# Attention regrouped into 36 phases of 1024 score columns a head, value products moved ahead of the transposes

## The chip, the cores and the metric

The kernel runs on one core of one Trainium2 chip. The metric is the time of one execution on the device, in microseconds. Instructions are issued in order on each engine: TensorE (matrix products and transposes, results to PSUM), VectorE (DVE), ScalarE (ACT), GpSimd (POOL) and SyncE (SP, which only starts transfers). Engines wait for each other by semaphores that count up.

## What is computed

The reference is one layer of a hybrid decoder for 1024 tokens of 1024 channels. The change touches the softmax and the value products of its two attention branches, which come between the input projection and the output projections:

```python
# branch B, causal, 8 heads; q, k of 64 + 32 channels
logits = einsum('bqhd,bshd->bhqs', q, k) * 96 ** -0.5
logits = where(s_idx <= t, logits, -inf)
y_b    = einsum('bhqs,bshd->bqhd', softmax(logits), v)      # v of 64 channels
# branch A, 8 query heads on 2 key heads, 64 channels; only the 256 keys that an indexer picks
logits = einsum('bqcgd,bqncd->bqcgn', q, k_sel) * 64 ** -0.5 - slope * distance
y_a    = einsum('bqcgn,bqncd->bqcgd', softmax(logits), v_sel)
merged = sigmoid(ga) * (y_a @ w_pa) + sigmoid(gb) * (y_b @ w_pb)
```

In the kernel branch A is dense and causal too: a table `sc` of what is to be subtracted holds the distance, and a huge number where a key isn't picked.

## The kernel before

The tokens are eight blocks of 128. Query block i sees i + 1 key blocks, `KEYS[i]` = 128 (i + 1) columns. Heads go in pairs p = 0 to 3; e = 0, 1 is the head in the pair, and the two heads' score products run in the two halves of TensorE's rows. A *step* n is one (branch, query block i, pair p). `STEPS` lists 64 of them, first 32 of branch B, then 32 of branch A; block 4 alternates with block 3, then 5 with 2, 6 with 1, 7 with 0:

```python
ORDER = [(TT - 1 - g, g) for g in reversed(range(TT // 2))]
STEPS = [(br, i, p) for br in "BA" for big, small in ORDER for p in range(PAIRS) for i in (big, small)]
```

For each step five things happen:

- **scores** (`scores_b` L2507 and L2511: five products per head; `scores_a` L2528: three) into two PSUM banks a head, in pieces of at most 512 columns;
- **reduction** on DVE (L1921): it writes scores minus mask into a buffer `prob` in SBUF and gives the row maximum; a short TENSOR_SCALAR (L1923 in B, L1926 in A) makes of it `shift`, and counts `shift_ready`. From then on the score banks are free;
- **exponential** on ACT (L1430), in place in `prob`, counted by `prob_ready`;
- **transposes** (`turn_probs`, L2544): 128 x 128 each, into units of up to four in a ring of three PSUM banks (`RING`), each unit counted by `turned`; ACT (L1394) or DVE (L1882, `copy_turned`) copies each unit to `prob_t`. A unit needs the one three before it to be copied;
- **value products** (`sum_values`, L2558), one per key block and head, which need all copies of their step; they count `pv_done`, and ACT takes the result out of PSUM (L1413, `take_y`).

TensorE's loop n issues scores(n), then transposes(n-1), then value products(n-2). DVE's loop n does both heads' reductions of n, then its copies of n-1. ACT's loop n does `take_y`(n-3) and then, for each head, its copy of n-1 and its exponential of n. There are four `prob` buffers, two for the even steps and two for the odd, so that a reduction of step n needs the transposes of step n-2.

Some work is laid into the same loops at given n: the split of `ka` into a high and a low part (`KA_SPLIT_AT`, ACT L1435 and DVE L1933) and of the queries `qa` of each set of blocks (`QA_SPLIT_AT`, L1439 and L1938), the inverse of branch B's sums (`INV_B`, `turn_inverse` L2569), and its spreading over the heads with the scaling of `yb` (`SPREAD_B`, four times: `spread_inverse` L2580 on TensorE, `scale_y` L1899 on DVE; they use the same ring). The same for branch A comes after the last step, `turn_inverse("A")` inside loop N + 1. Then the output products begin (L2282, `yb_hi`).

Of the kernel before, what the change touches and what calls it, by code (L numbers as in the profile page):

```python
# [22 lines left out]
P = 128  # L23
# [4 lines left out]
ALU = mybir.AluOpType  # L28
# [3 lines left out]
HEADS, HEAD_DIM = 8, 64  # L32
# [66 lines left out]
def build(nc, x, p, positions, g_mix, w_in, g_cq, w_uq, g_ckv, w_ukv, w_pa, w_pb, w_out, g_mlp, w_ff1, w_ff2,  # L99
# [36 lines left out]
    with ctx:  # L136
# [84 lines left out]
        PROB_AT = [(0, S), (4, S), (8, HALF), (10, HALF)]  # L221
        prob_b = [at(f"prob_b{j}", T + o * K, [n]) for j, (o, n) in enumerate(PROB_AT)]
        prob_a = [at(f"prob_a{j}", NX + (12 + o) * K, [n]) for j, (o, n) in enumerate(PROB_AT)]
        prob_tb = [at(f"prob_tb{j}", R1 + o * K, [n]) for j, (o, n) in enumerate(PROB_AT)]
        prob_ta = [at(f"prob_ta{j}", NX + o * K, [n]) for j, (o, n) in enumerate(PROB_AT)]
# [41 lines left out]
        max_c = col("max", 4)  # L267
        shift_c = col("shift", 4)
        fin_c = rstd_c = max_c
# [337 lines left out]
        NB = N // 2  # L607
        BANK_BLOCKS = HALF // P
# [32 lines left out]
        def turn_units(n):  # L641
            return [(e, half, UNIT_AT["turn", n, e, half]) for e in range(2)
                    for half in range(2) if ("turn", n, e, half) in UNIT_AT]
# [4 lines left out]
        def tiles_of(i, half):  # L648
            return (0, min(BANK_BLOCKS, i + 1)) if half == 0 else (BANK_BLOCKS, i + 1)
# [16 lines left out]
        KA_SPLIT_AT = 8  # L666
        QA_SPLIT_AT = [NB - 6, NB + 4, NB + 11, NB + 17]

# [4 lines left out]
        def prob_of(n, e):  # L673
            return (prob_b if STEPS[n][0] == "B" else prob_a)[2 * (n % 2) + e]

        def prob_t_of(n, e):
            return (prob_tb if STEPS[n][0] == "B" else prob_ta)[2 * (n % 2) + e]

# [12 lines left out]
        def y_steps(br, p):  # L691

            return 1 + max(n for n, (b, _, q) in enumerate(STEPS) if (b, q) == (br, p))

# [2114 lines left out]
```

## Time and profile before

| | |
|---|---|
| median of 3 runs | 1650.67 us (1650.38 to 1651.82) |
| the profiled execution | 1650.06 us, of which its span is 1648.3 us |
| mean granted TensorE clock | 0.996 of full |
| TensorE busy over the span | 97% |
| attention, branch B | about 433 to 580 us |
| attention, branch A | about 580 to 706 us |

The span runs from the first to the last instruction of the profile; 1.76 us of the execution lie around it. The profile has one row for each instruction or run of like instructions, with its start, its length and the idle time of its engine before it, and what ended it. A matmul's length is longer than its place in the pipeline: the distance from one start to the next is its cost. PEld rows are the weight loads that go before each matmul; they show those distances best.

### The profile page before, as it was taken

What the parts mean: (1) busy time and instruction counts of PE and PEld (TensorE: products, weight loads), DVE (VectorE), ACT (ScalarE), POOL (GpSimd) and SP (SyncE); (2) the same over time, 40 slices, a digit from 0 to 9 for tenths busy, and PEclk for the clock granted to TensorE, in tenths of its full rate; (3) what the DMA queues carried; (4) which work ended last, traced back from release to release, by engine and by line L of the source; (5) the groups of instructions that cost most, each with busy time, mean ns of one, the idle gap of its engine ahead of it and who ended that gap; (6) DMA issues with size and microseconds to landing.
All of it is one profiled execution on the core that took longest, in us unless ns stands there. A gap on an engine that the chain in (4) does not pass through costs nothing.

```text
span 1648.3 us, 23187 instructions
## 1 busy us (share of the span) xinstructions
PE 1596.7 (97%) x8576; PEld 1296.1 (79%) x8576; DVE 1201.2 (73%) x1851; ACT 699.9 (42%) x1151; POOL 637.1 (39%) x397
## 2 busy tenths in 40 slices
PE   6999999999999999999999999999999999999997
PEld 5778888787777777778888788888878888888786
DVE  7679999982656677754354777776699999898445
ACT  5432422323566677621144443343354444444223
POOL 2222532213200002012213545445589888885230
PEclk9999999999999999999999999999999999999999
DMA  5312223243300010203442354555494544422112
GB/s 164 93 39 58 96 77 102 90 126 82 90 1 2 1 40 2 78 25 131 168 137 89 119 169 141 160 171 160 155 338 170 204 163 166 141 90 64 45 58 102
DMA packets 115240, 177.46 MB, mean 108 GB/s; under 512 B 19104, under 2 KB 73376, under 8 KB 115008
## 3 DMA queue, kind: packets, MB, share of 16 engines
q1 hardware_dynamic: 111296, 162.44, 30.2%
q10 hardware_dynamic: 3680, 13.63, 2.2%
q8 instruction: 64, 1.05, 0.3%
q14 instruction: 40, 0.33, 0.1%
q0 software_dynamic: 160, 0.02, 0.0%
HBM read 123.24 MB, written 49.68 MB: 105 GB/s over the span
## 4 chain that ended last, share of the span: by engine, by line
PE 87%; DVE 7%; ACT 3%; issue 2%; POOL 1%; DMA 1%; SPq 0%; ACTq 0%; DVEq 0%
PE ps L2282 35%; PE ps L2718 18%; PE ps L2677 17%; PE ps L2544 3%; PE ps L2558 2%; PE ps L2507 2%; PE ps L2528 2%; PE ps L2423 2%; DVE prob_a L1921 1%; PE ps L2362 1%; PE ps L2330 1%; DVE prob_b L1921 1%; PE ps L2511 1%; PE ps L2641 1%; PE ps L2384 1%
## 5 line engine op out<-in xcount | busy, mean ns | idle before, releaser
L1037 POOL TENSOR_TENSOR w_lo<-w_raw,w_hi 128x1024 fp32r<-128x1024 f32 x67 | 166.1, 2480 | 481.9 <-ACT w_hi L1187 481.9
L1106 POOL TENSOR_TENSOR a_lo<-s_raw,a_hi 128x512 fp32r<-128x512 f32 x128 | 189.8, 1490 | 95.2 <-ACT a_hi L1466 94.8
L1187 ACT ACTIVATE w_hi<-w_raw 128x1024 fp32r<-128x1024 f32 x67 | 70.9, 1059 | 343.0 <-PE ps L2282 275.3
L2677 PE MATMUL ps<-b_hi,a_hi 128*128 128x512 f32 x448 | 175.3, 391 | 3.7 <-POOL a_lo L1106 1.7
L2718 PE MATMUL ps<-b_hi,a_hi 128*128 128x512 f32 x448 | 174.5, 390 | 2.4 <-DVE h L2155 2.4
L2677 PE MATMUL ps<-b_hi,a_lo 128*128 128x512 f32 x448 | 174.4, 389 | 0.0
L2677 PE MATMUL ps<-b_lo,a_hi 128*128 128x512 f32 x448 | 174.3, 389 | 0.0
L1106 POOL TENSOR_TENSOR a_lo<-f_raw,a_hi 128x512 fp32r<-128x512 f32 x96 | 136.8, 1439 | 97.1 <-ACT a_hi L1466 97.0
L2718 PE MATMUL ps<-b_lo,a_hi 128*128 128x512 f32 x448 | 174.3, 389 | 0.0
L2718 PE MATMUL ps<-b_hi,a_lo 128*128 128x512 f32 x448 | 174.3, 389 | 0.0
L2282 PE MATMUL ps<-n_hi,w_hi 128*128 128x512 f32 x544 | 168.3, 391 | 2.4 <-ACT rel L1247 1.3
L1769 DVE TENSOR_SCALAR_CACHE_REDUCE tested<-sc,bar_i 128x384 bf16<-128x384 f32 (+2 forms) x192 | 169.0, 942 | 1.7 <-POOL sc L1052 0.6
L2282 PE MATMUL ps<-n_hi,w_lo 128*128 128x512 f32 x544 | 167.5, 389 | 0.0
L2282 PE MATMUL ps<-n_lo,w_hi 128*128 128x512 f32 x544 | 167.4, 389 | 0.0
L2155 DVE TENSOR_TENSOR h<-h,ps 128x512 f32<-128x512 f32 x224 | 142.8, 677 | 23.4 <-PE ps L2718 23.0
L2105 DVE TENSOR_TENSOR b_lo<-b_lo,b_hi 128x512 fp32r<-128x512 f32 x112 | 143.5, 1321 | 0.1
L2282 PEld LDWEIGHTS ps<-n_hi,w_hi 128*128 128x128 f32 x544 | 101.8, 188 | 25.2 <-ACT rel L1247 1.7
L2282 PEld LDWEIGHTS ps<-n_lo,w_hi 128*128 128x128 f32 x544 | 102.1, 188 | 21.2
L2282 PEld LDWEIGHTS ps<-n_hi,w_lo 128*128 128x128 f32 x544 | 102.1, 188 | 21.2
L1466 ACT ACTIVATE a_hi<-s_raw 128x512 fp32r<-128x512 f32 x128 | 78.7, 627 | 92.5 <-PE ps L2718 90.9
L2677 PEld LDWEIGHTS ps<-b_hi,a_hi 128*128 128x128 f32 x448 | 84.1, 188 | 23.3 <-POOL a_lo L1106 3.3
L2718 PEld LDWEIGHTS ps<-b_hi,a_hi 128*128 128x128 f32 x448 | 84.1, 188 | 21.0 <-issue 3.5
(356 smaller groups left out, 3224.4 us busy)
## 6 DMA issues: line engine op xcount, KB each, us to landing
f_raw<-in_w_ff_dram SPq DMA_DIRECT2D x64, 512.0 KB, 4.3
b_lo<-hid_scratch SPq DMA_DIRECT2D x112, 256.0 KB, 5.5
hid_scratch<-c_out SPq DMA_DIRECT2D x32, 512.0 KB, 3.7
w_raw<-in_w_in_dram SPq DMA_DIRECT2D x28, 512.0 KB, 3.7
hid_scratch<-t_out SPq DMA_DIRECT2D x15, 768.0 KB, 6.1
gates_scratch<-stage ACTq DMA_DIRECT2D x16, 512.0 KB, 3.4
sig_ab<-gates_scratch SPq DMA_DIRECT2D x8, 1024.0 KB, 5.9
x_tok<-in_x_dram SPq DMA_DIRECT2D x8, 512.0 KB, 10.1
```

The costliest lines, as they stand in the source:

```text
L1037: pool.tensor_tensor(lo_of(first)[:, :, :], w_raw[s][:, :, :], hi_of(first)[:, :, :].bitcast(F32), ALU.subtract).then_inc(lo_ready, 1)
L1106: pool.tensor_tensor(slot(a_lo, o), first_of(o), slot(a_hi, o).bitcast(F32), ALU.subtract).then_inc(a_lo_done, 1)
L1187: act.activation(hi_of(first)[:, :, :], w_raw[s][:, :, :], ACT.Copy).then_inc(hi_ready, 1)
L1466: act.activation(slot(a_hi, o), first_of(o), ACT.Copy).then_inc(a_hi_done, 1)
L1769: ins = dve.tensor_scalar(tested[:, at0:at0 + KEYS[i]], s_i, bar_f[:, f:f + 1], None, ALU.is_ge, ALU.add, accum_out=count_c[:, f:f + 1])
L1921: link(dve.tensor_tensor_reduce(prob_of(n, e)[:, 0:w], s, less, 1.0, LOWEST, ALU.subtract, ALU.max, top))
L2105: dve.tensor_tensor(b_lo[r][:, b, :], b_lo[r][:, b, :].bitcast(F32), b_hi[r][:, b, :].bitcast(F32), ALU.subtract).then_inc(hid_lo_done, 1)
L2155: dve.tensor_tensor(h[k][:, part], h[k][:, part], pair_bank(w, name, ab), ALU.add).then_inc(added, 1)
L2282: last = pe.matmul(bank(4 * half + 2 * j + t)[0:w, :], wm, xm[:, t * HALF:(t + 1) * HALF], start=(n == 0 and a), stop=(n == total - 1 and ...
L2544: last = pe.transpose(bank(u % RING)[:, (k - k0) * P:(k - k0 + 1) * P], prob_of(n, e)[:, k * P:(k + 1) * P], ident[:, :])
L2677: last = pe.matmul(unit_bank(u, PLACE[name]), w[o % NS][:, j, :], x[j][:, b, :], start=name in ("P1", "P2", "P5") and j == 0 and a, stop=j ...
L2718: last = pe.matmul(pair_bank(w, name, ab), x[(LAST + o) % NS][:, 2 * j + ab, :], y[r][:, b, :], start=name in ("P1", "P2", "P5") and j == ...
```

## The change

The work of a branch is cut into 18 *phases* of exactly eight key blocks (1024 score columns) a head, instead of 32 steps of one to eight. A phase has one or two *members* (query block, pair, first column). Blocks 4 and 2 (5 + 3 key blocks) share a phase, 5 and 1 (6 + 2), 6 and 0 (7 + 1); block 7 fills a phase alone; block 3 of two pairs (4 + 4) fills one. Reductions, exponentials and `take_y` still go by member. TensorE's loop n now issues scores(n), value products(n-2), transposes(n-1). ACT's loop n takes the exponentials of the second members after both of the first. There are three `prob` buffers of 1024 columns a branch, used in turn by head: `prob` of phase n, head e is number (2n + e) mod 3. The units of transposes come in the order (first half, e = 0), (first half, e = 1), (second half, e = 0), (second half, e = 1); ACT copies the first two, DVE the last two, always 512 columns. `shift` has eight columns instead of four and takes the maximum in place.

The core of the diff; left out are renamings in `scores_a` (as in `scores_b`) and the counts of a few waits outside the attention:

```diff
-        prob_b = [at(f"prob_b{j}", T + o * K, [n]) for j, (o, n) in enumerate(PROB_AT)]
-        prob_a = [at(f"prob_a{j}", NX + (12 + o) * K, [n]) for j, (o, n) in enumerate(PROB_AT)]
+        prob_b = [at(f"prob_b{j}", T + 4 * j * K, [S]) for j in range(3)]
+        prob_a = [at(f"prob_a{j}", NX + (12 + 4 * j) * K, [S]) for j in range(3)]
+        prob_tb = [at(f"prob_tb{j}", R1 + 4 * j * K, [S]) for j in range(4)]
...
-        max_c = col("max", 4)
-        shift_c = col("shift", 4)
+        shift_c = col("shift", 8)
...
-        ORDER = [(TT - 1 - g, g) for g in reversed(range(TT // 2))]
-        STEPS = [(br, i, p) for br in "BA" for big, small in ORDER for p in range(PAIRS) for i in (big, small)]
+        ORDER = [(4, 2), (5, 1), (6, 0), (7, 3)]
+        def members_of(set_):
+            big, small = ORDER[set_]
+            if set_ < len(ORDER) - 1:
+                return [[(big, p, 0), (small, p, KEYS[big])] for p in range(PAIRS)]
+            return [[(big, p, 0)] for p in range(PAIRS)] + [[(small, p, 0), (small, p + 1, KEYS[small])] for p in (0, 2)]
+        STEPS = [(br, set_, members) for br in "BA" for set_ in range(len(ORDER)) for members in members_of(set_)]
...
-        INV_B = NB + 4
+        INV_B = NB + 2
         SPREAD_B = [INV_B + 2 + p for p in range(PAIRS)]
         for n in range(1, N + 1):
-            br, i, p = STEPS[n - 1]
-            for e in range(2):
-                add_unit("act" if i >= BANK_BLOCKS or e == 0 else "dve", "turn", n - 1, e, 0)
-                if i >= BANK_BLOCKS:
-                    add_unit("dve", "turn", n - 1, e, 1)
+            for half in range(2):
+                for e in range(2):
+                    add_unit("dve" if half else "act", "turn", n - 1, e, half)
...
-        KA_SPLIT_AT = 8
-        QA_SPLIT_AT = [NB - 6, NB + 4, NB + 11, NB + 17]
+        KA_SPLIT_AT = 5
+        QA_SPLIT_AT = [NB - 4, NB + 2, NB + 6, NB + 9]
...
         def prob_of(n, e):
-            return (prob_b if STEPS[n][0] == "B" else prob_a)[2 * (n % 2) + e]
+            return (prob_b if n < NB else prob_a)[(2 * n + e) % 3]
...
-        YB_HI_AT = [NB + 11 + 2 * k for k in range(YT)]
+        YB_HI_AT = [NB + 8 + k for k in range(YT)]
...
+                if n < N and len(MEMBERS[n]) == 2:
+                    for e in range(2):
+                        exponents(n, 1, e)
...
+                for a, e in itertools.product(range(len(MEMBERS[n]) if n < N else 0), range(2)):
...
+                    top = shift = shift_c[:, m % 8:m % 8 + 1]
                     dve.wait_ge(s_ready[e], n + 1)
-                    if n % NB >= 2:
-                        dve.wait_ge(turned, turned_after(n - 2, e))
+                    before = 2 * n + e - 3
+                    if a == 0 and before >= 2 * (n // NB * NB):
+                        dve.wait_ge(turned, turned_after(before // 2, before % 2))
...
+            def scores_free(n, e, at0):
+                if n >= 1 and at0 == 0:
+                    pe.wait_ge(shift_ready, score_index(n - 1, 0, e) + 1)
+                if n >= 1 and at0 == HALF:
+                    pe.wait_ge(shift_ready, 2 * FIRST_M[n])
...
             def turn_probs(n):
                 for e, half, u in turn_units(n):
-                    pe.wait_ge(prob_ready, 2 * n + e + 1)
+                    pe.wait_ge(prob_ready, probs_at(n, e, half))
                     unit_free(u)
...
             for n in range(1, N + 2):
-                if n == 4:
+                if n == 2:
                     pe.wait_ge(q_moved, ROPE_MOVED[1])
...
                 if n == 1:
                     freed(pe, 0, values_free)
+                if n >= 2:
+                    sum_values(n - 2)
                 if 1 <= n <= N:
                     turn_probs(n - 1)
                 if n == INV_B:
                     turn_inverse("B")
                 if n in SPREAD_B:
                     spread_inverse("B", SPREAD_B.index(n))
                 if n == N + 1:
                     turn_inverse("A")
-                if n >= 2:
-                    sum_values(n - 2)
```

`score_index(n, a, e)` numbers the reductions in their order, `FIRST_M[n]` is the number of members before phase n, `turned_after(n, e)` the count at which all units of that phase and head are transposed. So the first head of a phase may be reduced once the second head of the phase two before is transposed, and its second head once the first head of the phase just before is.

## Rows read from the trace of the kernel before

**Rows 1.** The page's first part: busy us of each engine, its share of the span, instructions.

```profile
PE 1596.7 (97%) x8576; PEld 1296.1 (79%) x8576; DVE 1201.2 (73%) x1851; ACT 699.9 (42%) x1151; POOL 637.1 (39%) x397
```

**Rows 2.** Windows over the two halves of the attention: start:end, length, busy us of each engine.

```profile
433.00:580.00 147.00, 137.56 (x1345) 108.40 (x1344) 84.75 (x243) 95.76 (x216) 4.70 (x2) 0.98 0.08 21
580.00:706.00 126.00, 118.73 (x1205) 91.14 (x1204) 89.78 (x260) 90.44 (x221) 9.86 (x5) 1.00 0.11 35
```

**Rows 3.** Waits in the attention, 433 to 706 us: who waited for whom, total, times, longest.

```profile
DVE prob_b L1921 <- PE ps L2511: 45.3, 29, 2.8
...
DVE prob_a L1921 <- PE ps L2528: 20.8, 25, 1.7
```

**Rows 4.** Timeline of branch A, TensorE's lines: start us, us, engine, line, operation.

```profile
657.17 0.50 PE L2528 MATMUL ps<-ka_hi,qa_hi 64*128 64x512 f32 x2
...
657.74 0.40 PE L2528 MATMUL ps<-ka_hi,qa_lo 64*128 64x512 f32 x2
...
657.97 0.33 PE L2528 MATMUL ps<-ka_hi,qa_hi 64*128 64x384 f32 x2
...
658.59 0.42 PEld L2544 LDWEIGHTS ps<-ident,prob_a 128*128 128x128 f32 x4 [0.26 <-issue]
...
659.18 1.51 PEld L2558 LDWEIGHTS ps<-prob_ta,va 128*64 128x64 f32 x28 [0.17 <-issue]
...
661.29 0.18 PEld L2528 LDWEIGHTS ps<-ka_hi,qa_hi 64*128 64x128 f32 x1 [0.25 <-DVE cols L1926]
...
661.84 1.18 PEld L2544 LDWEIGHTS ps<-ident,prob_a 128*128 128x128 f32 x11
...
664.37 0.50 PE L2528 MATMUL ps<-ka_hi,qa_hi 64*128 64x512 f32 x2
```

**Rows 5.** The same stretch, VectorE's lines.

```profile
658.70 1.09 DVE L1921 CUSTOM_DVE_ANT_0 prob_a<-ps,sc 128x896 f32<-128x896 f32 x1 [1.38 <-PE ps L2528]
...
659.95 1.09 DVE L1921 CUSTOM_DVE_ANT_0 prob_a<-ps,sc 128x896 f32<-128x896 f32 x1
...
661.08 0.15 DVE L1926 TENSOR_SCALAR cols<-cols 128x1 f32<-128x1 f32 x1
...
661.84 0.42 DVE L1921 CUSTOM_DVE_ANT_0 prob_a<-ps,sc 128x256 f32<-128x256 f32 x1 [0.25 <-PE ps L2528]
...
662.42 0.42 DVE L1921 CUSTOM_DVE_ANT_0 prob_a<-ps,sc 128x256 f32<-128x256 f32 x1
...
663.96 0.56 DVE L1882 COPY prob_ta<-ps 128x384 f32<-128x384 f32 x1 [0.43 <-PE ps L2544]
```

**Rows 6.** Timeline of branch B, VectorE's lines around a reduction of 1024 columns.

```profile
546.34 0.21 DVE L1923 TENSOR_SCALAR cols<-cols 128x1 f32<-128x1 f32 x1
...
549.89 0.69 DVE L1882 COPY prob_tb<-ps 128x512 f32<-128x512 f32 x1 [0.19 <-PE ps L2544]
```

**Rows 7.** First scores of step 1, first of branch A, first product after the attention.

```profile
441.70 0.18 PEld L2507 LDWEIGHTS ps<-kn_hi,qn_hi 64*128 64x128 f32 x2 [0.35 <-issue]
...
578.78 0.19 PEld L2528 LDWEIGHTS ps<-ka_hi,qa_hi 64*128 64x128 f32 x2 [0.17 <-issue]
...
705.80 0.30 PEld L2282 LDWEIGHTS ps<-yb_hi,w_hi 128*128 128x128 f32 x2 [0.17 <-issue]
```

**Rows 8.** Timeline around the split of ka, step 8 of the kernel before.

```profile
478.34 2.29 DVE L1933 TENSOR_TENSOR ka_lo<-ka,ka_hi 128x2048 fp32r<-128x2048 f32 x1 [2.40 <-ACT ka_hi L1435]
...
481.41 0.28 PEld L2507 LDWEIGHTS ps<-kn_hi,qn_hi 64*128 64x128 f32 x1 [1.12 <-DVE cols L1923]
```

**Rows 9.** Windows of 1 us behind it; PEclk is the granted clock behind POOL's.

```profile
482.00:483.00 1.00, 1.00 (x5) 0.78 (x6) 0.73 (x3) 1.00 (x4) 0.00 (x0) 0.50 0.00 0
...
488.00:489.00 1.00, 1.00 (x22) 0.83 (x18) 0.33 (x1) 1.00 (x4) 0.00 (x0) 1.00 0.00 0
```

**Rows 10.** The last transposes of the kernel, and a window among them.

```profile
1631.19 3.71 PE L2784 MATMUL ps<-ident,h 128*128 128x128 f32 x32
...
1638.00:1640.00 2.00, 1.52 (x12) 1.29 (x13) 1.93 (x5) 1.97 (x5) 0.00 (x0) 1.00 0.97 391
```

More of the change, by code:

```diff
@@ L641, in turn_units, with score_index, probs_at @@
         def turn_units(n):
-            return [(e, half, UNIT_AT["turn", n, e, half]) for e in range(2)
-                    for half in range(2) if ("turn", n, e, half) in UNIT_AT]
+            return [(e, half, UNIT_AT["turn", n, e, half]) for half in range(2) for e in range(2)]
         def turned_after(n, e):
             return 1 + max(u for e2, _, u in turn_units(n) if e2 == e)
-        def tiles_of(i, half):
-            return (0, min(BANK_BLOCKS, i + 1)) if half == 0 else (BANK_BLOCKS, i + 1)
+        def score_index(n, member, e):
+            return 2 * (FIRST_M[n] + member) + e
+        def probs_at(n, e, half):
+            last = max(a for a, (_, _, c0) in enumerate(MEMBERS[n]) if c0 < (half + 1) * HALF)
+            return score_index(n, last, e) + 1
         HI_ORDER = [("qi", 0), ("qn", 0), ("qn", 1), ("kr", 0), ("qr", 0), ("qn", 2), ("qn", 3), ("qr", 1)]
@@ L1410, in take_y, with exponents @@
             def take_y(n):
-                br, i, p = STEPS[n]
                 act.wait_ge(pv_done, n + 1)
-                act.activation(y_of(br)[:, p, i * P:(i + 1) * P], bank(PV_BANK)[:, 0:P],
-                               ACT.Copy).then_inc(y_copied, 1)
+                for a, (i, p, _) in enumerate(MEMBERS[n]):
+                    last = act.activation(y_of(STEPS[n][0])[:, p, i * P:(i + 1) * P], bank(PV_BANK)[:, a * P:(a + 1) * P],
+                                          ACT.Copy)
+                last.then_inc(y_copied, 1)
+            def exponents(n, a, e):
+                br = STEPS[n][0]
+                i, p, c0 = MEMBERS[n][a]
+                m, hd = score_index(n, a, e), 2 * p + e
+                act.wait_ge(shift_ready, m + 1)
+                prob = prob_of(n, e)[:, c0:c0 + KEYS[i]]
+                act.activation(prob, prob, ACT.Exp, bias=shift_c[:, m % 8:m % 8 + 1],
+                               scale=q_norm[:, i:i + 1] if br == "B" else SLOPES[hd],
+                               accum_out=sums_of(br)[:, i, hd:hd + 1]).then_inc(prob_ready, 1)
             for n in range(N + 3):
@@ L2539, in turn_probs @@
                 for e, half, u in turn_units(n):
-                    pe.wait_ge(prob_ready, 2 * n + e + 1)
+                    pe.wait_ge(prob_ready, probs_at(n, e, half))
                     unit_free(u)
-                    k0, k1 = tiles_of(STEPS[n][1], half)
-                    for k in range(k0, k1):
-                        last = pe.transpose(bank(u % RING)[:, (k - k0) * P:(k - k0 + 1) * P],
-                                            prob_of(n, e)[:, k * P:(k + 1) * P], ident[:, :])
+                    for k in range(BANK_BLOCKS):
+                        at0 = half * HALF + k * P
+                        last = pe.transpose(bank(u % RING)[:, k * P:(k + 1) * P], prob_of(n, e)[:, at0:at0 + P], ident[:, :])
                     last.then_inc(turned, 1)
             def sum_values(n):
-                br, i, p = STEPS[n]
+                br = STEPS[n][0]
                 for _, _, u in turn_units(n):
```

134 lines of the change are left out of this document (61 added, 73 removed).

## The prediction

> **What bounds the kernel now.** I read the page's first part, then windows over the attention, its waits, and the timeline of single steps. TensorE is busy 97% of the span [rows 1], and in the attention it stays the busiest engine: 137.6 of 147 us in branch B and 118.7 of 126 in A, where DVE has 89.8 and ACT 90.4 [rows 2]. So DVE waits for TensorE's scores, 45.3 us in B and 20.8 in A [rows 3], and TensorE waits little. But "busy" includes the drain of matmuls. The timeline shows what a step costs TensorE: a pair of blocks, nine key blocks a head, takes 664.37 - 657.17 = 7.20 us in A [rows 4]. Its own work by distances between starts is less. 28 weight loads of value products take 1.51 us, 0.054 each; 11 transposes take 1.18, 0.107 each; a score product of both heads takes 657.97 - 657.74 = 0.23 for 512 columns and, from 657.97 to 658.59 less the 0.10 of a change of kind, three of 384 in 0.52, 0.175 each [rows 4]. For 256 and 128 columns I estimate 0.12, between a load's 0.107 and the (661.84 - 661.29 - 0.10)/3 = 0.15 that a stretch of 256 with its start took. At a change of kind (scores, transposes, value products) 0.10 to 0.17 us goes idle. Work of the pair: scores 1.57, 18 transposes 1.93, 36 loads 1.94, in all 5.4; the remaining 1.8 us are six changes and short waits. This remainder is what fewer phases could save.
>
> **What the change removes.** The number of transposes, value products, pieces of scores and reductions is the same: per pair set, 5 + 4, 6 + 3, 7 + 2, 8 + 1 blocks become 5 + 3, 6 + 2, 7 + 1, 8, 4 + 4, with 48 pieces a branch either way. ScalarE and VectorE copy 512 columns always; that is no more than now in sum. Changes of kind fall from 3 x 64 to 3 x 36, and if nothing else bound, a phase would cost TensorE in A: scores 1.4, value loads 32 x 0.054 = 1.73, transposes 16 x 0.107 = 1.71, changes 0.45, in sum 5.3 us; in B, with five products, 6.3.
>
> **What it adds: a wait of VectorE within the loop.** The second head of phase n takes the `prob` buffer of the first head of phase n - 1, which must be transposed first. TensorE does this after the scores of n and after the value products of n - 2. Take V as the start of value products in loop n. The third unit of the transposes is the one waited for: value products 1.73, change 0.17, eleven transposes 1.18, and from the start of a unit's last transpose to DVE about 0.45 (the next scores start at 664.37; less 0.17, eight loads 0.43 and 0.17 the last transpose began near 663.5, and the copy of it starts at 663.96 [rows 4, 5]). The reductions after the first thus start at V + 3.5, where DVE had been free since about V + 1.3. Bounds 3.3 and 3.7.
>
> From there I follow DVE. The distance from one reduction to the next is 1.25 for 896 columns and 0.58 for 256 [rows 5], so 0.31 + 0.00105 w: 0.45, 0.58, 0.71, 0.85, 0.98, 1.12, 1.25, 1.38 for one to eight blocks; B has 0.02 more, its TENSOR_SCALAR being 0.21 instead of 0.15 [rows 5, 6]. TensorE is released 0.10 after the last distance in A (661.08 + 0.15, then 661.29), 0.15 in B. Two things hang on it.
>
> *Scores.* Pieces of phase n + 1 that begin at column 512 wait for all reductions of n; the tail behind that wait is five products in B, three in A. Loop time = 3.5 + three reductions + 0.15 + tail + 0.10. B: blocks 5 + 3: 3.5 + 2.46 + 0.15 + 1.45 + 0.10 = 7.66; 6 + 2: 3.5 + 2.34 + 0.15 + 1.2 + 0.1 = 7.29; 7 + 1: 7.41; 4 + 4: 3.5 + 2.61 + 0.15 + 1.15 + 0.1 = 7.5. Block 8 alone has one reduction (1.40), after which all of the second head's scores, 2.2, remain: 7.35.
>
> *Copies.* DVE copies units three and four after its reductions: 0.62 + 0.69 [rows 6] and 0.06 to TensorE, which needs them for the next value products. In A this is later than the scores: 5 + 3: 3.5 + 2.40 + 1.37 = 7.27; 6 + 2: 7.15; 7 + 1: 7.02; 4 + 4: 7.42. Block 8 alone is held by scores, 3.5 + 1.38 + 0.10 + 1.35 + 0.10 = 6.43.
>
> ScalarE fits in: after its first copy near V + 2.5 it has four exponentials and a copy, done by V + 7, and TensorE wants them at V' + 1.9, V' being the next V.
>
> **The sum.** Step 1's scores start at 441.70 [rows 7]; block 2's piece in phase 0 moves that by 0.3, as the wait for the value copies hides the rest. Scores(1) end at 444.6, the first third unit is through at 446.3, reductions 2.46, 0.15, tail 1.45: V of loop 2 is 450.4. Loops 2 to 17: 2 x 7.6 + 4 x 7.3 + 4 x 7.4 + 4 x 7.35 + 2 x 7.5 = 118.4. The split of `ka` (2.29 us on DVE, after ScalarE's high part [rows 8]) comes between two phases and delays the first reduction beyond V + 3.5: 1.6. Loop 18 starts at 570.4, its scores at 569. Now they start at 578.8 [rows 7]: B gains 10, of which 5 is a stall that the same split causes now.
>
> A: loop 18 needs no buffer back (`before` is below the branch), 5.4; three loops of 7.27; four of 7.15; four of 7.02; four of 6.43; two of 7.42: 124.4 with it. The inverse and the four spreads of B sit behind the transposes in the ring; their second unit needs DVE's copy of the third unit, which now comes at V + 3.5 + 2.3 + 0.7 = V + 6.5, and the next scores only after: 8.4 and 8.7 instead of 7.15 and 7.27, 6.4 in all. Last, value products of the last two phases, transposes, copies, then `turn_inverse("A")`: 7.8 (1.73 + 0.17 + 1.6 + 0.45, copies 1.0, value products 1.73, inverse 1.1). 570.4 + 124.4 + 6.4 + 7.8 = 709.0, against 705.8 now [rows 7]: **+3.2 us**. `qa` splits, `scale_y` and the inversion on DVE cost nothing: they lie between the copies and V + 3.5, where DVE waits 2 us a loop; without that cover each would cost its 0.7 to 1.3. SP's loads wait for counts reached as early as now. After the attention nothing changes.
>
> **The clock.** In the split's stall now, TensorE did little from 477.6 to 481.4, then was granted half clock: 0.50 in the window at 482, 1.00 again in that at 488 [rows 8, 9]. That was about 6.5 us, and a stretch at half clock costs at most half of itself. In the new loops with an inverse or a spread TensorE has nothing but two short instructions from V + 3.6 to V + 6.5, and in the `ka` loop little over 2.8 us. Six such places, each at least as empty as that stall; I count two to three drops of 2 us each, bounds 0 and 6 x 3.3. [...]
>
> Normal loops idle less at a time (1.0 + 0.8 + 0.4 us in A) but have 1.7 us of transposes before it. Transposes alone kept the clock at the end of the kernel: from 1631.19 on there is nothing else, and the window at 1638 has 1.00 [rows 10]. [...]
>
> **The rivals.**
> 1. *The clock holds.* The sum alone: 1650.06 + 3.2 = 1653, no change that a measurement can tell (below 0.2%, 3.3 us). For it: in A now it stayed at 1.00 [rows 2].
> 2. *Faster: the buffer is not what holds.* If the third unit were through before DVE ends its first reduction (V + 1.3), phases would cost 6.3 and 5.3: 16 x 1.1 + 17 x 1.7 = 46 us less, near 1607. The point from which it decides: at a gate of V + 3.5 every loop is bound by it; at V + 3.25 the sum is already 8 us lower, 1645. Against it: the order of the three parts on TensorE fixes the gate by work that I priced from rows.
> 3. *Half clock through much of the attention.* At half clock a loop's gate comes 1.4 later and its tail 0.7 to 1: if the 17 loops of A ran so, +35, near 1690.
> 4. *Nothing lost in the special loops*, because the ring's units are free earlier than I count: -6, near 1652 with the clock drops.
>
> **How the numbers follow.** The likeliest: the sum with two to three drops, 1650.06 + 3.2 + 5 = 1658.3; the profiled execution is 0.6 below the median of the runs, which I ignore: 1658. Chances: forecast 0.45, clock holds 0.20, ring free 0.10, faster 0.13, half clock 0.12. The gate's bounds are worth +-6 us over 33 loops. The range 1642 to 1675 leaves out the ends of rivals 2 and 3. Forecast alone: 1651 to 1668. Faster 0.16 (rival 2 and the low end of 1 and 4), same 0.24, slower 0.60.
>
> **What would show it.** Right: in A a loop of 7.0 to 7.3 us from value products to value products; each second head's reduction waits about 2 us for a transpose (L2544's counterpart), some 65 us over the attention; scores on TensorE released by DVE's TENSOR_SCALAR, value products by DVE's copy; B's scores end about 10 us earlier, the first output product 3 to 8 later; half clock only near 475 to 510 or 590 to 640. Wrong: loops of 6.3 and 5.3, TensorE waiting for nothing, or a clock below 1.00 in plain loops.

## The result and the profile after

| | before | after |
|---|---|---|
| median of 4 runs each | 1650.53 us (1650.37 to 1651.82) | 1677.16 us (1675.74 to 1679.02) |
| ratio | | 1.016, 95% interval 1.0143 to 1.0178 |
| span of the profiled execution | 1648.3 us | 1675.5 us |
| mean granted TensorE clock | 0.996 | 0.991 |

The change makes the kernel 26.6 us slower. The direction of the prediction was right; the size (1658) was not, and the time lies past the end of the range (1675).

The first part of the page after, against [rows 1]: TensorE's busy time is 3 us more, but its share falls from 97 to 95%.

```profile
PE 1599.9 (95%) x8576; PEld 1303.9 (78%) x8576; DVE 1200.5 (72%) x1827; ACT 688.4 (41%) x1127; POOL 636.9 (38%) x397
```

Windows over branch B and branch A (columns as in [rows 2]). In A the engine is busy for 130 of 161.5 us, and the clock has come down to 0.94.

```profile
433.00:571.50 138.50, 128.49 (x1292) 102.97 (x1290) 81.98 (x222) 86.11 (x194) 4.73 (x2) 1.00 0.08 22
571.50:733.00 161.50, 129.85 (x1257) 103.10 (x1257) 92.98 (x260) 87.85 (x218) 9.71 (x5) 0.94 0.08 27
```

The first output product, against the last row of [rows 7]:

```profile
732.81 0.30 PEld L2294 LDWEIGHTS ps<-yb_hi,w_hi 128*128 128x128 f32 x2
```

It comes 732.81 - 705.80 = 27.0 us later: the whole loss lies in the attention.

The waits of the attention, 433 to 735 us, against [rows 3]. L1932 is the reduction, L2565 the transposes, L1404 ScalarE's copy of them, L1935 and L1938 the short instruction behind a reduction, L2580 the value products, L1420 `take_y`, L1895 VectorE's copy.

```profile
ACT prob_ta L1404 <- PE ps L2565: 64.5, 19, 7.0
ACT prob_tb L1404 <- PE ps L2565: 51.3, 17, 3.7
DVE prob_a L1932 <- PE ps L2565: 48.9, 17, 4.1
...
DVE prob_b L1932 <- PE ps L2565: 35.1, 17, 2.7
...
PEld ps L2527 <- DVE cols L1935: 15.2, 24, 1.0
...
PE ps L2580 <- ACT ya L1420: 6.9, 5, 2.4
PE ps L2580 <- DVE prob_ta L1895: 5.9, 5, 3.5
...
PE ps L2580 <- ACT yb L1420: 3.2, 2, 1.9
```

VectorE's reductions wait for transposes, 48.9 + 35.1 = 84 us, where they waited for scores before. ScalarE's copies wait for transposes for 116 us; it is the other engine on which a loop can hang. And TensorE's value products wait for ScalarE's `take_y`, 6.9 + 3.2 = 10.1 us in seven waits, a pair that the prediction doesn't have. In the kernel before, 433 to 706 us, the same wait (L2558 for L1413) is next to nothing:

```profile
PE ps L2558 <- ACT ya L1413: 0.7, 2, 0.5
```

In what follows V is the start of a loop's value products, as in the prediction, and the *gate* is the wait of the second head's reduction for its `prob` buffer, which the third unit of transposes ends. One loop of branch B, from value products to value products, is 544.29 - 536.69 = 7.60 us:

```profile
536.69 1.73 PEld L2580 LDWEIGHTS ps<-prob_tb,vb 128*64 128x64 f32 x32 [0.35 <-issue]
...
538.59 1.29 PEld L2565 LDWEIGHTS ps<-ident,prob_b 128*128 128x128 f32 x12 [0.17 <-issue]
...
540.26 1.23 DVE L1932 CUSTOM_DVE_ANT_0 prob_b<-ps,mask 128x1024 f32<-128x1024 f32 x1 [2.20 <-PE ps L2565]
...
541.80 0.18 PEld L2527 LDWEIGHTS ps<-kn_hi,qn_hi 64*128 64x128 f32 x1 [0.98 <-DVE cols L1935]
...
543.02 0.42 ACT L1420 ACTIVATE yb<-ps 128x128 f32<-128x128 f32 x2
...
544.29 1.29 PEld L2580 LDWEIGHTS ps<-prob_tb,vb 128*64 128x64 f32 x24 [0.35 <-issue]
```

The second head's reduction starts at V + 3.57 after a wait of 2.20 us for the third unit of transposes (predicted V + 3.5), TensorE's next scores are released 1.54 later, and the tail takes 2.49. This is the predicted loop, 0.25 longer. `take_y` is done at 543.44, 0.85 before the value products: it fits in here.

Once in B it does not. ScalarE's part of the split of `ka` stands before `take_y`, and the value products wait 1.90 us for that; the loop is 9.38 us instead of 7.6:

```profile
480.82 1.90 ACT L1450 ACTIVATE ka_hi<-ka 128x2048 fp32r<-128x2048 f32 x1
...
483.18 1.97 PE L2580 MATMUL ps<-prob_tb,vb 128*64 128x128 f32 x32 [1.90 <-ACT yb L1420]
```

In branch A it often doesn't. Two loops between 645.8 and 663.3 us:

```profile
645.83 1.84 PEld L2580 LDWEIGHTS ps<-prob_ta,va 128*64 128x64 f32 x32
...
648.60 0.60 ACT L1404 ACTIVATE prob_ta<-ps 128x512 f32<-128x512 f32 x1 [5.62 <-PE ps L2565]
...
652.66 1.04 ACT L1462 ACTIVATE yb_hi<-yb 128x1024 fp32r<-128x1024 f32 x1
...
653.61 0.41 ACT L1420 ACTIVATE ya<-ps 128x128 f32<-128x128 f32 x2
...
654.17 1.97 PE L2580 MATMUL ps<-prob_ta,va 128*64 128x128 f32 x32 [1.43 <-ACT ya L1420]
...
660.88 1.04 ACT L1454 ACTIVATE qa_hi<-qa_raw 128x1024 fp32r<-128x1024 f32 x1
661.82 1.04 ACT L1462 ACTIVATE yb_hi<-yb 128x1024 fp32r<-128x1024 f32 x1
...
662.77 0.41 ACT L1420 ACTIVATE ya<-ps 128x128 f32<-128x128 f32 x2
```

ScalarE's first copy comes at V + 2.77. Its exponentials stand behind it and are done at V + 6.9; then come `yb_hi` (0.95 from start to start, a filler job at the end of the loop) and only then `take_y`, done at V + 8.2. The value products of the next loop need `take_y`: it empties the one bank that they write to. They start 0.12 later. With a second filler (`qa_hi`) the loop is 9.2 us.

### The profile page after: what moved, and what is told of

Its sections match the earlier page's. It is cut to its first block, busy times and chain, and to the rows that moved or that the text cites. A ratio compares the mean times of both kernels' runs of the same rounds, so it can differ in the third digit from the quotient of the medians.

```text
span 1675.5 us, 22963 instructions
## 1 busy us (share of the span) xinstructions
PE 1599.9 (95%) x8576; PEld 1303.9 (78%) x8576; DVE 1200.5 (72%) x1827; ACT 688.4 (41%) x1127; POOL 636.9 (38%) x397
## 4 chain that ended last, share of the span: by engine, by line
PE 87%; DVE 8%; ACT 3%; issue 1%; POOL 1%; DMA 1%; SPq 0%; DVEq 0%; ACTq 0%
PE ps L2294 34%; PE ps L2740 17%; PE ps L2699 17%; PE ps L2580 4%; PE ps L2565 3%; PE ps L2527 2%; PE ps L2435 2%; DVE prob_a L1932 2%; PE ps L2374 1%; DVE prob_b L1932 1%; PE ps L2342 1%; PE ps L2531 1%; PE ps L2549 1%; PE ps L2663 1%; ACT prob_a L1430 1%
```

## The experiments

Medians are of four executions of each kernel (ten for e7), timed beside the kernel before, whose medians were 1649.7 to 1651.6 us. *Loop n* is measured in the one profiled execution of each kernel, from the start of value products to the start of the next.

| | kernel | median, us | ratio to before |
|---|---|---|---|
| | after the change | 1677.2 | 1.0160 |
| e1 | `take_y` early | 1669.6 | 1.0114 |
| e2 | inverse and spreads behind the scores | 1672.9 | 1.0132 |
| e3 | transposes head by head | 1672.0 | 1.0128 |
| e4 | four buffers in branch A | 1668.2 | 1.0102 |
| e5 | the gap of a spread filled | 1677.1 | 1.0150 |
| e6 | e1, e2 and e4 together | 1639.7 | 0.9935 |
| e7 | e6, head 0's transposes before the value products | 1646.6 | 0.9979 |
| e8 | phases with the old order | 1629.8 | 0.9876 |
| e9 | before, with the new order | 1718.7 | 1.0414 |
| e10 | e8 and the spreads of e2 | 1617.2 | 0.9794 |
| e11 | e9 and `take_y` early | 1658.3 | 1.0051 |
| e12 | e10, transposes head by head | 1615.8 | 0.9795 |

The 95% intervals of the ratios are 0.001 to 0.0021 to either side. Those of e2, e3 and e5 overlap with that of after (1.0143 to 1.0178), so their gains are not clear of noise; those of e1 and e4 are.

**e1: `take_y` early.** In ScalarE's loop n:

```diff
-                if n >= 3:
-                    take_y(n - 3)
+                if 2 <= n < N + 2:
+                    take_y(n - 2)
```

> Only ScalarE's take_y is moved: its loop n takes the value products of phase n - 2 out of PSUM at its start, before its first copy, instead of those of n - 3. Theory: value products(n) wait in the changed kernel for take_y(n - 1), which stands in ScalarE's queue behind the exponentials, the high part of yb and the high part of qa of the loop before; in the loops of branch A with the high parts of yb (starts at 645.8 to 681.3) that is what holds, 8.2 to 9.8 us instead of 7.1, and a stretch at half clock follows from it. Then these four loops become 7.0 to 7.2, the first loop of A gets up to 1.5 shorter, the rest keeps its 7.4 to 7.7: 6 to 9 us less than the changed kernel, about 1669. Rival: the wait shown there is only the last of several, DVE's copies end as late; then at most 1 us less.

Measured: 7.6 us less than after. Loop 18 falls from 7.01 to 5.73, loops 26 to 29 from 8.31, 9.15, 9.79, 8.21 to 7.74, 7.12, 7.12, 7.12. So those loops did hang on `take_y`. In B most loops are what they were, but the cost of the split of `ka` changes its place: loop 5 falls from 9.38 to 7.41, and loops 6 and 7 rise from 7.58 and 7.65 to 9.75 and 8.07, now behind VectorE's part of the split and at a clock of 0.88 and 0.94. The other loops hang on something else, or on two things at once.

**e2: the inverse and the spreads out of the ring's end.** `turn_inverse` and `spread_inverse` of loop n are issued in loop n + 1 right behind the scores, before `sum_values`, where their units are long free.

> Only TensorE's order is changed: the inverse of B's sums and its four spreads are issued one loop later, after that loop's scores and before its value products, with the same order in the ring. Theory: behind the transposes they hold up the next scores until DVE has copied the third unit, and the idle stretch brings the clock to half; five loops of A take 9.1 and 10.0 us for that. Moved, they wait for nothing: the five become 7.3 to 7.6 and the clock stays at full in them, 10 to 13 us less, about 1665. Rival 1: the clock falls in them anyway, since a plain loop idles enough; then 3 to 6 less. Rival 2: DVE's scaling of yb, now later, delays the next reduction beyond the gate; then 0 to 3 less.

Measured: 4.3 us less than after. Loops 22 and 23 fall from 10.0 to 7.44 and 7.41, 24 and 25 to 8.2 and 8.9, but loops 27 and 28 grow from 9.15 and 9.79 to 10.54 and 11.06, at a granted clock of 0.82 and 0.73. The stall is gone from the spreads. They give 8.1 us in this execution; loops 27, 28 and 36 take 3.9 of it back at a clock that is lower than after's. The 10 to 13 us expected did not come.

**e3: transposes head by head.** `turn_probs` and the ring's order go over e outside and over the halves inside, so the first head's buffer is free one unit (four transposes) earlier.

> Only the order of the transposes' units is changed: both halves of the first head, then both of the second (ScalarE still copies first halves, DVE second halves). The first head is then free after two units instead of three, 0.43 us earlier. Theory: the second head's reduction, gated by that, heads the chain of every loop: 33 loops x 0.43 = 14 us less, less what the spread and yb loops don't pass on: 9 to 14 less, about 1666. Rival: TensorE's other waits set the loop, 0 to 3 less.

Measured: 5.2 us less, where 9 to 14 were expected. Plain loops of B go from 7.5 to 7.8 down to between 7.2 and 7.4, loops 19 and 21 of A from 7.39 to 7.0. Four transposes are 4 x 0.107 = 0.43 [rows 4], and 0.2 to 0.4 of them arrive: these loops follow the gate. A's stop at 7.0, where the next thing holds them. Much of the rest the clock took: this trace has 34.1 us at the lower clock in the attention, after has 20.5 (loops 6, 20, 24 to 28 and 30 are at 0.81 to 0.85). At what such time costs in e5 below, 0.38 us each, I estimate 5 us.

**e4: a fourth buffer in branch A.**

```diff
-        prob_a = [at(f"prob_a{j}", NX + (12 + 4 * j) * K, [S]) for j in range(3)]
+        prob_a = [at(f"prob_a{j}", o, [S]) for j, o in enumerate((NX + 12 * K, NX + 16 * K, NX + 20 * K, R1 + 32 * K))]
...
-                    before = 2 * n + e - 3
+                    before = 2 * n + e - (3 if n < NB else 4)
```

`prob_of`, left out here, counts modulo 4 in A.

> Only the prob buffers of branch A are four instead of three, in room that branch B has left; both reductions of a phase then need only the phase two before. B keeps three. Theory: B unchanged at 7.5 to 7.8 us a loop. In A the gate of 3.6 us goes: plain loops fall from 7.4 (6.7 for block 7 alone) to 5.3 to 6.3, held by TensorE and DVE alone or by ScalarE's take_y; spread and inverse loops by 1 to 2 each, yb loops little. 15 to 25 us less in all, about 1657. Rival: the order on ScalarE holds as long in A: 3 to 8 less.

Measured: 8.9 us less, not 15 to 25. With the buffers' gate away VectorE's reductions no longer wait for transposes in A, and yet loops 19, 21, 22 and 23 don't fall below 7.02. What holds them is in the trace of e4, rows of ScalarE and TensorE from loop 19 into loop 20 (the second copy and three of four exponentials left out):

```profile
585.98 0.60 ACT L1404 ACTIVATE prob_ta<-ps 128x512 f32<-128x512 f32 x1 [2.80 <-PE ps L2565]
...
589.18 0.61 ACT L1430 ACTIVATE prob_a<-prob_a,cols 128x384 f32<-128x384 f32 x1
...
589.77 0.43 ACT L1420 ACTIVATE yb<-ps 128x128 f32<-128x128 f32 x2
...
590.35 1.97 PE L2580 MATMUL ps<-prob_ta,va 128*64 128x128 f32 x32 [1.25 <-ACT yb L1420]
...
593.00 0.60 ACT L1404 ACTIVATE prob_ta<-ps 128x512 f32<-128x512 f32 x1 [2.80 <-PE ps L2565]
```

It is a circle, and it closes without VectorE: value products (n-2) come before transposes (n-1); ScalarE's copy waits for those (2.80 us); its four exponentials stand behind the copy; `take_y` stands behind them; the value products of the next loop wait for it (1.25 us). From copy to copy the circle is 593.00 - 585.98 = 7.02 us. So A has two holders almost level, the buffers' gate with 7.4 and this circle with 7.0. To take away the gate alone gives 0.4 us a loop (e4), `take_y` alone next to nothing in a plain loop (7.39 to 7.36 in e1).

**e5: the gap filled.** Fourteen transposes of the identity stand in front of the first half of each spread, into the bank that this half then overwrites. They fill 1.51 us in which TensorE would otherwise wait for VectorE's copy before the second half.

> The changed kernel with 14 transposes of a constant put in front of the first part of each of the four spreads of branch B, into the bank that the spread is about to overwrite. They add work and take no wait away: 14 x 0.107 = 1.5 us, where TensorE waits 1.5 us for DVE's copy anyway. Theory: the four spread loops take 10.0 us instead of 8.4 only since the clock falls to half behind the gap. If 1.5 us of transposes keep the clock, the four become 8.4 to 8.6 at clock 1.00 and the kernel is 5 to 6 us faster than the changed one, about 1671. Rival: the gap before and behind is still long enough, or transposes don't keep the clock: no change, 1677, clock 0.84 in those loops.

First the gap and the clock in the kernel after. One spread's loop, and windows of it (PEclk behind POOL's column, as in [rows 9]):

```profile
610.61 0.18 PEld L2602 LDWEIGHTS ps<-inv_t,spread 16*128 16x128 f32 x1 [0.98 <-ACT prob_ta L1404]
...
611.56 1.29 DVE L1895 COPY prob_ta<-ps 128x512 f32<-128x512 f32 x2
612.30 0.28 PEld L2602 LDWEIGHTS ps<-inv_t,spread 16*128 16x128 f32 x1 [1.51 <-DVE prob_ta L1895]
```

```profile
606.00:612.00 6.00, 4.34 (x49) 3.46 (x47) 3.09 (x13) 3.38 (x8) 0.00 (x0) 1.00 0.02 4
612.00:616.00 4.00, 3.70 (x21) 2.76 (x23) 2.14 (x5) 0.94 (x6) 0.00 (x0) 0.50 0.00 0
616.00:620.00 4.00, 4.00 (x39) 3.83 (x40) 1.10 (x3) 0.06 (x1) 0.00 (x0) 0.65 0.00 0
```

TensorE waits 0.98 us for ScalarE's copy, issues one half of the spread, waits 1.51 for VectorE's. Then the scores of the next phase start at half clock (0.50 in the window at 612), and it is back at full clock only at 618.8 (0.99 in the microsecond from there), towards the end of the value products behind them. All four spread loops are like this in length, 10.06, 9.96, 10.03 and 9.96 us, and in mean clock, 0.81 to 0.84, but not in where the clock is low. There are three stretches at 0.50, not four: 612.0 to 618.8, 625.6 to 629.1 and 642.7 to 646.1 us. Behind loop 23's spread the scores still run at full clock and the value products that begin loop 24 at half; behind loop 24's spread, with the same waits, nothing drops:

```profile
623.75 0.18 PEld L2602 LDWEIGHTS ps<-inv_t,spread 16*128 16x128 f32 x1 [1.52 <-DVE prob_ta L1895]
...
625.84 3.27 PEld L2580 LDWEIGHTS ps<-prob_ta,va 128*64 128x64 f32 x32 [0.20 <-issue]
...
633.85 0.18 PEld L2602 LDWEIGHTS ps<-inv_t,spread 16*128 16x128 f32 x1 [1.52 <-DVE prob_ta L1895]
...
635.87 1.73 PEld L2580 LDWEIGHTS ps<-prob_ta,va 128*64 128x64 f32 x32
```

Measured in e5: those four loops are 8.74, 8.69, 8.71, 8.83, all with clock 1.00, 5.0 us less in sum. So the 13.4 us at half clock in these loops cost 5.0, 0.38 for each. 8.7 is close to the 8.4 predicted for them without a loss of clock.

But the total is unchanged: the ratio is 1.0150 against 1.0160, with intervals that overlap. Loops 17, 18 and 20 now have clocks of 0.93, 0.86 and 0.86, loop 28 has 0.75 (10.78 us against 9.79) and loop 30 has 0.81 (8.76 against 7.10). The two kernels differ from loop 22 on, so loops 17 to 20 run what they ran before. So the place of a drop is not fixed by the instructions of a loop. Nor is the amount fixed by the kernel: the ten executions of e7 go from 1642.8 us at a mean clock of 0.997 to 1650.7 at 0.992, and the four of e5 from 1672.0 at 0.995 to 1677.8 at 0.991. Whether the total of e5 stayed because drops moved there, or because its executions happened to have more of them, stays open. With the filler none of the four spread loops has a drop, where after, e1 and e8, with waits of 1.0 to 1.2 and 1.3 to 1.5 us there, have one behind 11 of 12.

e5's fillers are nothing but transposes, and with 1.51 us of them in place of the wait the clock was 1.00 in all four loops.

**e6: the three mends together.** e1, e2 and e4.

> The early take_y, the spreads behind the scores, and four prob buffers in branch A together. Theory: in A three waits stand almost level, DVE's gated chain (7.4), take_y behind ScalarE's queue (7.0, which is what held the four buffers alone) and the spreads with the clock. With all three gone A's loops fall to 5.5 to 6.2, with those of the high parts up to 6.5; B stays at 7.6. From 145 us for loops 18 to 35 to about 108, so 1640 for the kernel (1636 to 1648). Rival: ScalarE's own work (4 exponentials, 2 copies, take_y, about 5.5 us a loop) with its wait for the transposes makes a fourth wait of the same size; then A's loops stay above 6.7 and the kernel at 1655 or more.

Measured: 1639.7 us, 37.5 us less than after, where the three alone gave 7.6, 4.3 and 8.9, in sum 20.8. Plain loops of A fall to 5.7, and 30 to 34 to 5.54; B's plain loops stay at 7.4 to 7.8. This is what two level holders and a changing clock look like: each mend alone only uncovers the next holder. Of the 16.7 us that the three give beyond their sum, part is the clock: 3.4 us at the lower level in the attention here, 20.5 in after and 23.9, 20.5 and 17.1 in e1, e2 and e4. By 0.38 us each I estimate 5 to 8 us of it. Loops 19, 22 to 25 of after and e6: 7.39 and 5.71; 10.06, 9.96, 10.03, 9.96 and 6.25, 6.69, 7.04, 8.60.

**e7: head 0's transposes before the value products.** e6, head by head, and TensorE's loop is scores(n), transposes(n-1) of head 0, value products(n-2), transposes of head 1.

> The same as e6, and TensorE transposes the first head of phase n - 1 in front of the value products of n - 2, the second head behind them. Theory: B's loops are held by the gate of 3.6 us; with the first head's 8 transposes right behind the scores it comes at 1.5, and B's loops fall from 7.6 to 6.4 to 6.8, TensorE's own work and four changes of kind: 14 to 18 us less than e6, near 1625. In A nothing is gained, a change of kind more costs 0.1 to 0.2 a loop. Rival: the transposes then wait for the first head's exponentials (its second member's are last in ScalarE's queue), and B's loops stay above 7.2.

Measured (here 10 runs, 1642.8 to 1650.7): 6.9 us more than e6, not 14 to 18 less. B is shorter (7.0 to 7.5), A's plain loops are longer (6.1 to 6.5) and those with extra work are 7.2 to 9.7. The early `take_y` now stands before ScalarE's copy of head 0 and waits for value products that come later, and the ring runs full behind it:

```profile
593.39 0.45 ACT L1420 ACTIVATE ya<-ps 128x128 f32<-128x128 f32 x2 [2.24 <-PE ps L2582]
...
594.47 0.63 PE L2567 MATMUL ps<-ident,prob_a 128*128 128x128 f32 x4 [0.54 <-ACT prob_ta L1404]
```

This cause is read from the trace and was not tested by a run of its own. The clock is 1.00 in each of its loops, although some of them are as long as 9.7 us.

**e8: phases with the old order.** In TensorE's loop `sum_values(n - 2)` stands last again; everything else is as after.

```diff
-                if n >= 2:
-                    sum_values(n - 2)
                 if 1 <= n <= N:
                     turn_probs(n - 1)
...
                 if n == N + 1:
                     turn_inverse("A")
+                if n >= 2:
+                    sum_values(n - 2)
```

> The changed kernel with the order of before on TensorE: transposes of n - 1 directly behind scores of n, value products of n - 2 last. Phases, buffers and units stay. Theory: the gate comes 1.75 + 0.17 us earlier, at 1.7 behind the scores, and the transposes wait for the exponentials instead, which ScalarE ends 0 to 1 us before the scores are done; loops of 6.3 to 7.2 in B, 6.3 to 7.3 in A. The kernel at 1650 to 1662, 15 to 27 less than changed: the order, not the phases, is what costs. Rival: the phases cost (three buffers, longer members); then 1670 or more.

Measured: 1629.8 us, 47.4 less than after and 1.24% faster than before, 20 us below the range that I had expected. Plain loops of B are 6.44 to 6.73, of A 5.53 to 5.7. Two rows of value products in A are 5.54 apart, with the transposes before them and nothing waited for:

```profile
658.60 1.73 PEld L2580 LDWEIGHTS ps<-prob_ta,va 128*64 128x64 f32 x32 [0.17 <-issue]
...
662.09 1.29 PEld L2565 LDWEIGHTS ps<-ident,prob_a 128*128 128x128 f32 x12 [0.36 <-issue]
...
664.14 1.73 PEld L2580 LDWEIGHTS ps<-prob_ta,va 128*64 128x64 f32 x32 [0.17 <-issue]
```

The phases are good, and the price of one on TensorE is close to what the prediction worked out for it, 6.3 and 5.3. Three buffers are enough in this order: the reductions wait for transposes for 10 us in both branches, where in after it was 84. The spreads still stall it: loops 22 to 24 are 10.1 at clock 0.83 (in this order the spread of phase n lies in loop n - 1, since the value products come behind it).

**e9: the new order without the phases.** The kernel before, with `sum_values(n - 2)` ahead of `turn_probs(n - 1)`. It has four buffers.

> The kernel before the change with only TensorE's order changed: value products of step n - 2 in front of the transposes of step n - 1. Its four prob buffers (two for even steps, two for odd) and 64 steps stay. Theory: the order costs much only together with three buffers, since with four no reduction waits for the transposes of the step just before; what is left is the wait of value products for take_y behind ScalarE's queue, and scores held by DVE less than before. 1650 to 1662. Rival: the order alone costs what it costs in the changed kernel (the old order there gave 47 us); then 1680 or more.

Measured: 1718.7 us, 67 more than before. My theory had been that the order costs only where there are three buffers, and it fell here. The waits of that kernel, 433 to 775 us (L1394 copy, L2544 transposes, L1413 `take_y`, L2558 value products):

```profile
ACT prob_tb L1394 <- PE ps L2544: 77.8, 35, 5.1
ACT prob_ta L1394 <- PE ps L2544: 77.6, 37, 4.7
...
PEld ps L2558 <- issue: 67.4, 55, 3.4
...
PE ps L2558 <- ACT ya L1413: 30.8, 22, 2.3
...
PE ps L2558 <- ACT yb L1413: 24.8, 17, 3.1
```

It is the circle of e4 again, now in both branches: the value products wait 55.6 us for `take_y`. Three rows of its timeline show the end of one round:

```profile
563.42 1.23 ACT L1430 ACTIVATE prob_b<-prob_b,cols 128x1024 f32<-128x1024 f32 x1
...
564.65 0.26 ACT L1413 ACTIVATE yb<-ps 128x128 f32<-128x128 f32 x1
...
565.05 0.66 PE L2558 MATMUL ps<-prob_tb,vb 128*64 128x128 f32 x8 [1.55 <-ACT yb L1413]
```

**e11: e9 with `take_y` early**, to tell that circle from another cause.

> The kernel before with the value products ahead of the transposes (the order that alone cost 67 us), and in ScalarE's loop n take_y(n - 2) at its start in place of take_y(n - 3). Theory (the circle: value products wait for take_y, which stands behind the exponentials of the loop before, which stand behind the copy of transposes that come behind the value products): the wait of value products for take_y goes, some 55 us of it in the attention, and the time falls from 1718.7 to between 1655 and 1675; what stays over 1650 is the wait of ScalarE's exponentials for the copy alone. Rival (the order costs by another wait, take_y is only the last one seen; the copies or the buffers hold the loop): value products start as late as before, now behind the copies of the transposes, and the time stays over 1700.

Measured: 1658.3 us, 60.4 less than e9. The wait of value products for `take_y` is gone from the trace, and 8.5 us of the 67 remain (ratio to before 1.0051, interval 1.0034 to 1.0068). What they are stays open. It isn't the wait of transposes for ScalarE's copies: in B that is 5.0 us here and 5.1 in the kernel before.

So on the kernel before, the place of `take_y` behind the exponentials is 60 of the 67 us that the order costs, what its waits do to the clock included (mean 0.983 in e9, 0.996 in e11).

**e10: the old order, and the spreads behind the scores.**

> The phases with the old order of TensorE (e8), and in addition the inverse and the spreads of branch B behind the next loop's scores. Theory: e8 has five loops of 7.2 to 10.1 us where plain ones take 5.6, for the ring's wait and the half clock behind it; moved they fall to 5.7 to 6.5: 14 to 18 us less than e8, about 1613. Rival: the stall moves on to DVE's scaling, or the clock falls for another reason: 1620 to 1630.

Measured: 1617.2 us, 2.06% faster than before and 12.6 less than e8, where 14 to 18 were expected. Over both branches the clock is 1.00, and TensorE is busy for 132 of 133 us in B:

```profile
433.00:566.00 133.00, 132.01 (x1413) 110.19 (x1413) 92.87 (x253) 95.78 (x219) 4.72 (x2) 1.00 0.11 29
566.00:667.00 101.00, 96.35 (x1065) 78.88 (x1062) 81.70 (x225) 76.42 (x190) 9.60 (x4) 1.00 0.11 38
```

Spread loops take 6.8, 6.8, 8.5 and 6.9, where e8 had up to 10.1. Here e2's edit gives 12.6 us, where on the kernel after it gave 4.3: in the profiled execution there is no other loop in which the clock falls.

**e12: e10 head by head.**

> The fastest kernel so far (phases, transposes ahead of value products, inverse and spreads right behind the scores) with the transposes in the order head 0, both halves, head 1, both halves. If something of the buffer's wait is left in it, the second head's reduction starts one unit of transposes earlier and the time falls from 1617.2 by 3 to 8 us. If TensorE is now bound by its own work, no change beyond 2 us, or a loss of some us, as in the run that combined this order with three mends, because ScalarE's second copy now comes before VectorE's first.

Measured: 1615.8 us (1615.2 to 1616.7) against 1617.2 (1615.8 to 1617.8) of e10; the two ratios, 0.9795 and 0.9794, don't tell them apart, and the loops agree to 0.04 but for one (7.63 against 7.70). What the same edit gave in B in e3, 0.2 to 0.4 a loop, was the buffer's wait, and in this order there is little of it (8.6 us over both branches in e10).

## Why the prediction was wrong

The prediction by its own stretches, the start of value products in loop 2 first:

| stretch | predicted | measured | difference |
|---|---|---|---|
| V of loop 2 | 450.4 | 450.87 | +0.5 |
| loops 2 to 17 (branch B) | 120.0 | 124.05 | +4.1 |
| loop 18 | 5.4 | 7.01 | +1.6 |
| loops 19 to 21, one with the inverse | 23.2 | 23.89 | +0.7 |
| loops 22 to 25, the spreads | 33.6 | 40.01 | +6.4 |
| loops 26 to 29 | 28.1 | 35.46 | +7.4 |
| loops 30 to 33 | 25.7 | 27.12 | +1.4 |
| loops 34, 35 | 14.8 | 15.01 | +0.2 |
| from there to the first output product | 7.8 | 9.39 | +1.6 |

In sum 23.8 us, of which the prediction had 5 as a lump for the clock: 18.8 too few, against 1677.2 - 1658 = 19.2 in the medians. The first row is met so well partly by luck: e2, e4 and e5 run the same instructions up to there and had 450.7 to 452.8.

**The step that failed** is the line "ScalarE fits in: ... done by V + 7, and TensorE wants them at V' + 1.9". The V + 7 was right (6.9 in the rows above). But the exponentials aren't what TensorE wants first. `take_y` stands behind them in ScalarE's queue, and with the value products moved to the front of the phase's work TensorE wants it at V', not after the transposes. In before it hardly shows (0.7 us), because there the transposes come in between. I followed the release of every buffer that the *new* units need, and not that of the bank which the *moved* instruction itself writes. Where a filler job (`qa_hi`, `yb_hi`, 0.94 each) lies between, the loop gets longer by it. The prediction put the `qa` splits at nothing, covered by VectorE's wait, and gave ScalarE's half of them and `yb_hi` no term at all; on VectorE the cover was there, on ScalarE it wasn't. Loop 18 and loops 26 to 29 lose 9 us; by e1, in which they are 5.73 and 29.1 together, `take_y` is behind 7.6 of them, partly with the clock of loop 28 (0.83). The 1.6 us for the split of `ka` came out at 1.8 (loop 5, 9.38 against 7.6), but by luck: the prediction has them on VectorE before the gate of the next loop, and in the trace they are `take_y` behind `ka_hi`.

**The clock** was the right mechanism, and its term was mis-sized: 5 us, for "two to three drops of 2 us". Three drops came behind the four spreads, 5.0 us together by e5 (40.01 against 34.97); that alone is the term. Two more came in loop 28 (clock 0.83, 1.6 us more than the like loop 29 with 1.00, 8.21) and in loop 36 (0.74), which I had not named: 1.6 and, at most, the 1.6 of the last stretch. In sum 6.6 to 8.2 us, where the term was 5. Time at half clock cost 0.38 of itself in the four spread loops (5.0 of 13.4 us); the half that I had put as the most was my estimate. Of the six places that I had named, three had a drop; loop 24's spread, the inverse (loop 20, 9.11 us) and the split of `ka` (loop 5, 9.38) kept 1.00.

**The gate** was right. Measured V + 3.57 against V + 3.5 in B, and 609.42 - 605.85 = 3.57 in A. B's loops are 7.55 to 7.79 (but for loop 5), predicted 7.3 to 7.7; most are 0.2 to 0.3 too long, of which, in the loop shown above, the gate is 0.07 and the tail 0.19 (2.49 from release to value products, predicted 2.30). That is the +4.1. e3 (one unit earlier, 0.2 to 0.4 less a loop) and e4 (VectorE's wait gone) show that it was the buffer. A plain loop of A is 7.39, predicted 7.27; those of block 7 alone (30 to 33) are 6.6 to 7.1, predicted 6.43. VectorE's waits for transposes are 84 us instead of "some 65".

**The spreads** at V + 6.5 were right too: 8.7 with full clock (e5), predicted 8.4.

**The rivals.** 1 (the clock holds) and 4 (nothing lost) did not happen. 3 (half clock through much) did not: B is at 1.00, plain loops of A as well. 2 (phases of 6.3 and 5.3 us, near 1607) is what the phases give in the old order, e8 with 6.44 to 6.73 and 5.54, and e10 gets to 1617. The point of decision that I gave for it was on the gate. There was a second one that I had not seen, since with the gate lifted in A (e4) the circle over ScalarE still holds 7.02.

**How the parts add up.** Phases alone: -20 us (e8), or -34 with the spreads moved (e10; what moving them would give on the kernel before was not tried). The moved value products: +47 on the phases, +67 on the kernel before. On the phases e6 gets 37.5 of those 47 back; in B, whose loops are still 7.4 to 7.7 against 6.5 in e8, VectorE's reductions still wait 34 us for transposes. That the three buffers are what holds them, 16 loops by about 1 us, was not tested: a fourth buffer in B was not tried. What else is open is what decides where the clock falls: in the profiled executions of after and of e1 to e5, five to eleven loops ran at 0.61 to 0.95, not always those with the longest waits. In those of e7, e10 and e12 no loop is below 1.00.

## What to carry to other kernels

When an instruction is moved ahead on one engine, ask first who must have emptied what *it* writes, and where that reader stands in its own queue; then follow the queue round until it closes. A circle through two in-order queues has a length of its own, and it can be level with the holder that you found; taking either away alone shows little (20.8 us for the three mends taken one by one, 37.5 together). Undo one half of a change with two parts before judging it: here one part is worth 20 to 34 us and the other costs more than that.

A filler job must not stand in front of an instruction that another engine waits for. `yb_hi` in front of `take_y` cost about 1 us a loop (8.2 to 8.3 us at full clock); with `take_y` early and `yb_hi` in the same place the loop is 7.12, 0.1 over what was predicted without it.

## What the runs showed of the hardware

Behind a wait of 1.0 to 1.2 us and one of 1.3 to 1.5 us, with one short product between them, the granted clock fell to 0.50 of full after three of four spreads and stayed at 1.00 after one; in e1 and e8 it fell to 0.50 after all eight. 32 value loads took 3.27 us in such a stretch and 1.73 outside. With fourteen transposes in the second of the waits it was 1.00 in all four loops (e5). The 13.4 us at 0.50 in the four loops cost 5.0 us. I had not expected how loosely the drops are tied to a place: loops 17, 18 and 20 of e5, which run the same instructions as after, had 0.86 to 0.93 where after has 1.00, and ten executions of one kernel (e7) had mean clocks of 0.990 to 0.997 and times from 1650.7 down to 1642.8 us. A wait of more than 1 us did not always bring a drop. In the profiled executions of e10, e12 and e7 every loop has 1.00: in e10 and e12 TensorE's weight loads wait once for more than 1 us, for 2.1, and in e7 three times, for 1.1, 1.2 and 2.8.
